# Multiplying the output gate's row into an expert's rows on GpSimd, ahead of their scatter, instead of on VectorE in the combine

## The reference, cut to what matters

```python
u = modulate(h_lat, mod_lat[3], mod_lat[4])
weights = softmax(top_v) * g_prob            # two experts of 32 for each token
y = lax.map(expert_block, (xin, block_e))    # hid = silu(x @ w_gate) * (x @ w_up); hid @ w_down
ffn_lat = zeros.at[row_tok].add(y * row_w)   # each token's two rows, weighted and summed
h_lat = layer_norm(DN_ALPHA * h_lat + mod_lat[5] * ffn_lat, ln_g, ln_b)
```

## Time and profile before

| what | value |
|---|---|
| median of 3 runs | 2576.6 us (2568.36 to 2577.54, mean 2574.2) |
| profiled execution | 2572.02 us, its span 2570.2 us |
| mean granted clock of PE | 0.968 of full speed |
| busy over the span | PE 94%, PEld 76%, DVE 63%, ACT 37%, POOL 10% |
| DMA | 437.51 MB, mean 170 GB/s |

### The profile page before, as it was taken

The page is one execution under the profiler, slowest core; times in us unless marked ns, Lnnn a source line. Parts: engine busy times, 40 slices in busy tenths (PEclk is TensorE's granted clock), DMA queues, the critical chain, the costliest instruction groups (busy, mean ns, idle before and its releaser), DMA issues. The chain is left out here.

```text
span 2570.2 us, 30487 instructions
## 1 busy us (share of the span) xinstructions
PE 2407.5 (94%) x11928; PEld 1950.9 (76%) x11928; DVE 1630.3 (63%) x1666; ACT 941.3 (37%) x1100; POOL 251.7 (10%) x234
## 2 busy tenths in 40 slices
PE   6999899799996989999999999999599999999994
PEld 2468778678885878788877888868588888888882
DVE  6453299533323763522984635668888889888976
ACT  5233301333321533101112100021277777777764
POOL 0000000000103310000000001100011212121210
PEclk8999999899998999999999999999799999999997
DMA  5431255212326222111111113533689999999975
GB/s 202 169 115 50 74 173 178 85 54 82 123 69 195 88 64 98 61 49 51 46 41 45 37 49 130 198 142 130 259 316 368 365 363 363 363 371 387 384 269 204
DMA packets 95120, 437.51 MB, mean 170 GB/s; under 512 B 16057, under 2 KB 28617, under 8 KB 80299
## 3 DMA queue, kind: packets, MB, share of 16 engines
q1 hardware_dynamic: 68330, 357.81, 37.5%
q0 software_dynamic: 26688, 78.30, 8.7%
HBM read 401.51 MB, written 55.51 MB: 178 GB/s over the span
## 5 line engine op out<-in xcount | busy, mean ns | idle before, releaser
L390 PE MATMUL ps<-uT_upper_rest,ring_rest 128*128 128x512 f32 x1296 | 513.0, 396 | 0.0
L390 PE MATMUL ps<-uT_upper_rest,mix_upper 128*128 128x512 f32 x768 | 307.6, 400 | 9.6 <-DVE mix_val L2342 5.3
L390 PE MATMUL ps<-uT_rest,mix_upper 128*128 128x512 f32 x768 | 306.5, 399 | 0.0
L390 PEld LDWEIGHTS ps<-uT_upper_rest,ring_rest 128*128 128x128 f32 x1296 | 244.8, 189 | 61.5
L390 PEld LDWEIGHTS ps<-uT_upper_rest,mix_upper 128*128 128x128 f32 x768 | 145.7, 190 | 47.1 <-DVE mix_val L2342 5.7
L390 PEld LDWEIGHTS ps<-uT_rest,mix_upper 128*128 128x128 f32 x768 | 145.7, 190 | 32.6 <-issue 0.5
L1774 ACT ACTIVATE mix_gates<-ps 128x1024 f32<-128x1024 f32 x24 | 24.7, 1027 | 384.3 <-PE ps L390 367.1
L1825 DVE TENSOR_TENSOR mix_prod<-mix_gates,ps 128x1024 f32<-128x1024 f32 x24 | 29.3, 1220 | 209.9 <-PE ps L390 209.9
L2873 PE MATMUL ps<-ex_u_raw_rest,uT_rest 128*128 128x256 f32 x560 | 157.5, 281 | 0.0
L390 PE MATMUL ps<-uT_upper_rest,xbc_upper 128*128 128x512 f32 x336 | 136.6, 407 | 7.6 <-DVE ring_rest L940 7.6
L2871 PE MATMUL ps<-ring_rest,uT_rest 128*128 128x256 f32 (+1 forms) x416 | 135.5, 326 | 3.1 <-DVE uT_rest L3236 2.4
(11 more groups left out here) (464 smaller groups left out, 5535.7 us busy)
## 6 DMA issues: line engine op xcount, KB each, us to landing
sb_spare<-in_ex_g SPq DMA_DIRECT2D x35, 2048.0 KB, 9.9
ex_u_raw<-in_ex_u SPq DMA_DIRECT2D x35, 2048.0 KB, 10.2
sb_merged<-in_ex_d SPq DMA_DIRECT2D x35, 2048.0 KB, 9.3
ring<-in_conv SPq DMA_DIRECT2D x32, 512.0 KB, 3.3
ring<-in_w_gate SPq DMA_DIRECT2D x32, 512.0 KB, 3.3
mix_piece<-in_w_late POOLq DMA_DIRECT2D x32, 512.0 KB, 5.4
ring<-in_w_ssd SPq DMA_DIRECT2D x21, 512.0 KB, 3.2
ring<-in_w_mod SPq DMA_DIRECT2D x16, 512.0 KB, 4.2
```

The costliest lines, as they stand in the source:

```text
L390: last = self.nc.tensor.matmul(out, weight, x[:, k, lo:hi], start=(k == 0 and n == 0), stop=(k == kt - 1 and n == 2))
```

## The change

`scatter` on POOL gets a multiply of `y` by the gate's row, in place in SBUF, and a wait for it. `residual` on DVE loses its multiply and the wait behind it, and adds `h_last` straight to the sum in PSUM. PE's wait for a free pair of banks is now for the sum with the residual.

```diff
 def scatter(i):
     pool.wait_ge(y_ready, i + 2)
+    nc.gpsimd.tensor_tensor(y, y, rows[:, 3, :], ALU.mult).then_inc(y_gated, 1)
+    pool.wait_ge(y_gated, i + 1)
     pool.indirect_dma_start(out=a["y_rows"], ...
 ...
 for t in range(TT):
     pe.wait_ge(diag_set, 2 * (t + 1))
     if t >= 4:
-        pe.wait_ge(mix_done, t - 3)
+        pe.wait_ge(summed, t - 3)
     pe.wait_ge(y_in[t], 32)
 ...
 v.wait_ge(mixed, t + 1)
-tt(acc, sum_banks(t), rows[:, 3, :], ALU.mult).then_inc(mix_done, 1)
-v.wait_ge(mix_done, t + 1)
 v.wait_ge(h_in[t], 16)
-stt(out=acc, in0=h_last[:, t, :], scalar=ALPHA, in1=acc, op0=ALU.mult, op1=ALU.add).then_inc(summed, 1)
+stt(out=acc, in0=h_last[:, t, :], scalar=ALPHA, in1=sum_banks(t), op0=ALU.mult,
+    op1=ALU.add).then_inc(summed, 1)
```

More of the change, by code:

```diff
@@ L2642, in stage_experts @@
         hid_mm, hid_cast, hidc_ready = sem("hid_mm"), sem("hid_cast"), sem("hidc_ready")
-        y_ready, y_out = sem("y_ready"), sem("y_out")
+        y_ready, y_out, y_gated = sem("y_ready"), sem("y_out"), sem("y_gated")
         picked_y = (u_raw[:, :, :].rearrange("p b (k n) -> p (b k) n", n=D), merged[:, :, :])
@@ L2652, in stage_experts @@
         out = [sem(f"out{n}") for n in range(RING)]
-        weights_set, diag_set, mixed, mix_done, summed, act_own, spread_in, var_ready, root, inverse, scaled, ready = (
-            sem(n) for n in ("weights_set", "diag_set", "mixed", "mix_done", "summed", "act_own", "spread_in", "var_ready",
+        weights_set, diag_set, mixed, summed, act_own, spread_in, var_ready, root, inverse, scaled, ready = (
+            sem(n) for n in ("weights_set", "diag_set", "mixed", "summed", "act_own", "spread_in", "var_ready",
                              "root", "inverse", "scaled", "ready"))
```

## The result

The changed kernel takes 2615.3 us (median of 4 runs, 2615.26 to 2621.02), the kernel before in the runs beside it 2575.0 us (median of 4, 2568.36 to 2577.54). The ratio is 1.0167, 95% interval 1.0146 to 1.0187: **slower by 1.7%**, where 2610 us (2590 to 2640) was forecast. The profiled execution took 2621.0 us with a span of 2619.2 us; it is the slowest of the four, the other three took 2615.3.

A forecast was written before the change was run, and what follows sets the result against it. The prediction took a loop of PE, DVE and ACT, with 0.6 us of slack at DVE, to bound the blocks. Blocks +42.2, last scatter +2.1 and combine -8.8 gave +35.5 us on 2574.2: 2610 us, range 2590 to 2640.

The forecast's parts named there:

- What bounds the blocks: Expert blocks: PE, DVE and ACT go round in a loop, with 0.6 us of slack for DVE in an 18.27 us period.
- Who holds whom, and where: Expert blocks: POOL's multiply enters behind chunk 2, holds DVE's chunk 3 for 1.84 us; 34 x 1.24 = +42.2 us.
- Rival 1: Expert blocks, chunk 2 to 3 boundary: DVE not held, or hold within the slack; 2567.5 us, no change; chance 0.14.
- The multiply's length: POOL's 128x1024 multiply takes 1.97 us, scaled by elements from the scan's 1.48 us for 128x768.
- The last scatter: Behind the last block: POOL's multiply lies on the path, 1.97 us and 0.1 for the wait, +2.1 us.
- The combine: Combine: DVE loses the multiply and its hand-over, 1.26 us in each of seven turns, -8.8 us.
- Rival 3: Combine does not shorten, since PE or ACT fills DVE's turn; 8.8 us stay, 2619 us; chance 0.06.
- Rival 2: Expert blocks: POOL misses the boundary, the scatter lands late, ACT's copy waits; +34 us more, 2644 us; chance 0.12.
- The cover that looked like 0.2 us at the worst: Expert blocks: the scatter lands at worst at 2233.8, and ACT wants `y` free at 2234.0, so the landing stays hidden.
- The total: Whole kernel: 42.2 + 2.1 - 8.8 = +35.5 us, added to the runs' mean of 2574.2 us, forecast 2610 us.
- The signs named beforehand: Rows expected in the profile after: multiply 35 times, chunk 3 4.1 us, period 19.5, PE idle 1.2 a block, scatter 2.3.

The follow-up runs named there:

- Five runs with five lengths: Changed kernel, and it with POOL's instruction replaced: one-input multiply, 512 columns, 768 columns, repeated second input; ratios to before 1.0167, 1.0008, 1.0033, 1.0104, 1.0113.
- the run with the multiply alone: Kernel before with POOL's multiply and its wait added ahead of each scatter, combine untouched; 2626.9 us, ratio 1.0222.
- the write without a read: Changed kernel with POOL's multiply replaced by a memset that clears 128x2048 of a dead tile; 2564.7 us, ratio 0.9967 to before.
- the run with the gather between: Changed kernel with ACT's copy behind chunk 5, POOL's order multiply, gather, scatter, and three gathers ahead of the blocks; 2572.6 us, ratio 1.0003 to before.
- the multiply twice: Changed kernel with POOL multiplying twice, one after the other, ahead of each scatter; 2699.0 us, ratio 1.0505 to before.
- 512 columns: Changed kernel with POOL multiplying 512 of the 1024 columns of `y`; 2580.9 us, ratio 1.0033 to before.
- the version with two tiles: The run with the gather between, but `y` alternates between two tiles and the last block's copy takes a third; 2566.0 us, ratio 0.9976 to before.

## Why the prediction was right, and where a term was off

**What bounds the blocks: right.** The loop of PE, DVE and ACT with its slack at DVE was read from one block, as 0.6 us. Five runs with five lengths give 0.63 or 0.64. What the working left out is that PE meets chunk 3 itself, 0.4 us a block; since PE comes late to the turn by as much, the sum is the same.

**Who holds whom, and where: right.** The multiply gets in at the boundary behind chunk 2, chunk 3 waits for its length less 0.13 us, and the chunks behind it stand in line. Rival 1 falls by chunk 3's hold and by the run with the multiply alone (1.0222); by the write without a read (0.9967) it would have been right of an instruction that only writes.

**The multiply's length: the step that was mis-sized.** "By elements 128x1024 takes 1.48 x 1024 / 768 = 1.97 us" should have been 2.34. The step failed less in the scaling than in the row that it scaled: the scan's multiply has a second input of one value for 64 columns, which the row's shape doesn't show but the kernel's line does. A full row of 768 columns takes 1.80 us, and 1024 columns with a repeated input 1.90. With 2.34 in its place, the forecast's own working gives 2.34 - 0.13 - 0.6 = 1.61 us and 34 x 1.61 = +54.7 us, where the trace has +53.6; it said +42.2. The estimate from the Trainium skill, "GPSIMD Engine Reference", section "Performance versus the Vector engine", 2.25 us and +51.7 us, was nearer; I set it aside for the row of this kernel, and that row was of another form.

**The last scatter: right but for the same length.** +2.4 us instead of +2.1. **The combine: right.** -8.83 us by the trace and -8.7 by the ratio of the run that has it alone, for -8.8; DVE's turn 3.97 us, as said. (PE's new wait is for the residual four turns back, `t - 4`, and not three; it was long done either way.) Rival 3 falls: DVE waits for nobody behind the second turn.

**Rival 2 did not come.** POOL did reach the boundary, with 0.25 us to spare, and the landing, for which 12.7 us by the median and 15.3 at worst had been taken over from before, took 7.6 and 9.3. The cover that looked like 0.2 us at the worst was wider. Where the wait for a landing did come, in the run with the gather between, it was of the forecast's kind: 35.3 us on ACT, of which the blocks' time shows 4.4.

**The total.** The sum by the rows, +47.2 us instead of +35.5, is off by the multiply's length all but alone: 11.4 us in the blocks and 0.3 at the end. The time forecast, 2610, is only 5.3 us below the median, since the medians differ by 7 us less than the rows' sum. Runs of one kernel lie 6 to 9 us apart, so that the total came so near is in part luck; by the rows the forecast was 11.7 us too low.

**The signs named beforehand.** Chunk 3 at 4.1 us was 2.29 + 2.21 = 4.50; the period of 19.5 was 19.85; PE's 1.2 us a block were about 1.0 of idle rows, though the period grew by 1.58 (PE's weight loads wait 1.1 us at the turn and 0.4 at chunk 3); the scatter's row of 2.3 us was 2.25 by the median (1.95 in the block shown). POOL's multiply was there 35 times, but 2.34 us alone and 2.59 in the blocks, for 2.0 and up to 2.3. PE's clock kept its 1.00 in the blocks, as said; with the multiply twice it did not.

## What to carry to other kernels

Work that is moved from a busy engine's last stage to an idle GpSimd, and that reads SBUF there, was free in these runs only where VectorE had no instruction with two SBUF inputs under way: read from VectorE's timeline which instructions stand at the moment at which GpSimd will ask, count how much slack the loop has, and charge everything above it once a round. When a duration is scaled from another row, take one with the same form of operands (a full row against a repeated value), not only the same operation. If the place is bad, move the request and not the work: here a later copy, a reordered queue and a second tile made the same multiply cost nothing in the blocks, but each of these steps uncovered the next wait, and it took all three to keep the gain. And before a price that held at several lengths is carried further, look at the granted clock there: with the multiply twice it was no longer 1.00 in the blocks.

## What the runs showed of the hardware that was not expected

- GpSimd's multiply by a constant, with one SBUF input, is longer alone than its multiply of two tiles (2.81 against 2.34 us for 128x1024) and yet holds VectorE for less (0.84 against 2.21 us).
- GpSimd's multiply by a repeated value takes 1.90 us for 128x1024, by a full row 2.34.
- The indirect DMA's instruction on GpSimd takes 1.00 to 1.05 us where VectorE has no instruction with two SBUF inputs, and mostly longer where it starts within one: 1.95 and 2.71 us in the rows shown, by the median 2.25 in the changed kernel and 3.03 in the run with the write without a read. It was not seen to hold VectorE: chunk 4 keeps its 2.29 us.
- The time from the scatter's issue to its landing fell from 12.7 to 7.6 us by the median when the scatter came about 3 us later in its block, and was 7.6 with the multiply alone too, but 12.1 with 512 columns, 12.1 with the write without a read, where it came 2 us later, and 11.8 in the version with two tiles. What sets it was not tried.
- With the multiply twice, when PE stood up to 2.2 us at once ahead of the turn of the second hidden half (0.9 in the changed kernel), its granted clock was 1.00 and 0.86 by turns from block to block; in the changed kernel it stayed at 1.00. That the stands are the reason is not shown.
